# Expert weights in longer runs: two neighbouring rows to a partition, and a step of two on the stationary side

## The reference

```python
gate = jnp.minimum(xb @ wg + bg, SWIGLU_LIMIT)
up = jnp.clip(xb @ wu + bu, -SWIGLU_LIMIT, SWIGLU_LIMIT)
glu = gate * jax.nn.sigmoid(SWIGLU_ALPHA * gate)
return ((up + 1.0) * glu) @ wd + bd
```

## Time and profile before

| | |
|---|---|
| median of 3 runs | 1285.4 us |
| lowest and highest run | 1281.82 and 1287.41 us |
| span of the profiled execution | 1284.3 us |
| TensorE, matmuls busy | 1223.1 us (95%) |
| TensorE, weight loads busy | 552.0 us (43%) |
| VectorE, ScalarE, GpSimd busy | 250.6, 183.5 and 19.8 us |
| moved by DMA | 455.34 MB, 355 GB/s over the span |
| queue of the large loads | 132080 packets, 446.73 MB |

### The profile page before, as it was taken

How to read it: one execution, slowest core, us unless ns; L and a number is a source line. 1 busy time by engine, 2 the same in 40 slices (tenths; PEclk the granted TensorE clock), 3 DMA queues, 4 the chain that set the end, 5 groups by cost and what they waited for, 6 DMA issues and landing times.

```text
span 1284.3 us, 15147 instructions
## 1 busy us (share of the span) xinstructions
PE 1223.1 (95%) x6020; PEld 552.0 (43%) x6020; DVE 250.6 (20%) x535; ACT 183.5 (14%) x305; POOL 19.8 (2%) x40
## 2 busy tenths in 40 slices
PE   6699999999999999999999999999999999999995
PEld 1388965543333334443333333333333333333332
DVE  1334571511111111111111111111111111111113
ACT  1122431201111111111111111111111111111111
POOL 3000000000000000000000000000000000000000
PEclk9599999969999999999999999999999999999998
DMA  9994359529999999999999999999999999999971
GB/s 316 333 331 140 118 202 360 197 110 373 398 407 406 406 407 405 403 409 408 405 407 406 405 408 403 405 404 410 405 404 408 407 406 406 407 408 406 405 303 33
DMA packets 135160, 455.34 MB, mean 355 GB/s; under 512 B 7967, under 2 KB 21299, under 8 KB 135014
## 3 DMA queue, kind: packets, MB, share of 16 engines
q1 hardware_dynamic: 132080, 446.73, 89.3%
q0 software_dynamic: 2064, 6.98, 1.6%
q10 hardware_dynamic: 998, 1.37, 0.4%
HBM read 453.35 MB, written 1.70 MB: 354 GB/s over the span
## 4 chain that ended last, share of the span: by engine, by line
PE 82%; ACT 3%; DVE 1%; issue 0%
PE bank L1431 53%; PE bank L1415 10%; PE bank L1424 5%; PE bank L1441 5%; PE bank L1406 3%; PE bank L1307 2%; ACT k_pool L623 1%; PE bank L1102 1%; ACT at_pool L615 1%; PE bank L1134 1%; PE bank L1109 1%; PE bank L1463 0%; PE bank L1375 0%; PE bank L1343 0%; DVE xres L1063 0%; DVE k_pool L1062 0%
## 5 line engine op out<-in xcount | busy, mean ns | idle before, releaser
L1431 PE MATMUL bank<-ring,at_pool 128*64 128x512 f32 x2048 | 456.1, 598 | 0.0
L1431 PEld LDWEIGHTS bank<-ring,at_pool 128*64 128x64 f32 x2048 | 141.9, 137 | 310.5 <-issue 310.5
L1431 PE MATMUL bank<-ring,k_pool 128*64 128x512 f32 x1024 | 226.8, 595 | 23.0 <-ACT k_pool L623 23.0
L1431 PEld LDWEIGHTS bank<-ring,k_pool 128*64 128x64 f32 x1024 | 70.7, 137 | 158.5 <-issue 127.9
L1415 PEld LDWEIGHTS bank<-keyT,rows 128*128 128x128 f32 x1056 | 123.7, 196 | 28.6 <-issue 28.6
L1005 DVE TENSOR_SCALAR k_pool<-bank 128x512 f32<-128x512 f32 x32 | 22.1, 692 | 578.9 <-PE bank L1431 578.9
L1415 PE MATMUL bank<-keyT,rows 128*128 128x64 f32 x1056 | 128.5, 281 | 0.0
L615 ACT COPY at_pool<-bank 128x512 f32<-128x512 f32 x33 | 19.3, 586 | 443.3 <-PE bank L1415 443.3
L1424 PE MATMUL bank<-kv_pool,cumT 32*64 32x512 f32 x256 | 69.6, 620 | 0.0
L1009 DVE TENSOR_SCALAR k_pool<-bank 128x512 f32<-128x512 f32 x32 | 22.1, 692 | 226.9 <-PE bank L1431 226.9
L1441 PE MATMUL bank<-d_pool,at_pool 64*128 64x512 f32 x264 | 65.6, 615 | 0.7 <-ACT d_pool L625 0.7
(11 more groups left out here) (300 smaller groups left out, 590.5 us busy)
## 6 DMA issues: line engine op xcount, KB each, us to landing
ring<-in_w_gate SPq DMA_DIRECT2D x128, 1024.0 KB, 9.5
ring<-in_w_up SPq DMA_DIRECT2D x128, 1024.0 KB, 8.7
ring<-in_w_down SPq DMA_DIRECT2D x128, 1024.0 KB, 7.4
ring<-in_w_mod SPq DMA_DIRECT2D x24, 1024.0 KB, 10.1
ring<-in_w_in SPq DMA_DIRECT2D x13, 1024.0 KB, 12.5
ring<-in_w_out SPq DMA_DIRECT2D x4, 1024.0 KB, 6.7
k_pool<-in_const_masks POOLq DMA_DIRECT2D x1, 1024.0 KB, 8.0
g<-in_b_mod POOLq DMA_DIRECT2D x2, 512.0 KB, 12.3
```

Source lines behind the costliest of these rows:

```text
L1431: ins = mm(bank[CAP * half:CAP * (half + 1), :], lhsT(2 * r + kk), w[:, kk, 512 * half:512 * (half + 1)], start=m == 2 and r == 0 and kk = ...
```

## The change

A chunk of 256 rows is spread over the partitions in another way: partition p receives rows 2p and 2p + 1, which lie next to each other in memory, so that it reads one run of 8192 bytes where it read two of 4096. The slot then holds, as its two tiles, the even and the odd rows of the chunk. The two factors of each product have to agree on which features a tile holds, so the stationary side of the gather and of the transposes takes every second column of its 256: tile k is columns 256 * (k // 2) + k % 2, in steps of two. The number and the sizes of all transfers and instructions stay.

```diff
+        def pair_tile(k):
+
+            return slice(256 * (k // 2) + k % 2, 256 * (k // 2 + 1), 2)
+
...
                     sp.wait_ge(chunks_used, used(cidx - RING, count))
                     sp.dma_start(ring[:, expert_slot(cidx), :].rearrange("p (k n) -> p k n", k=2),
                                  w[0, bass.ds(e, 1), 256 * (cidx % 4):256 * (cidx % 4 + 1), :]
-                                 .rearrange("a (k p) n -> p (a k) n", p=P)).then_inc(slot_loaded[expert_slot(cidx)], 16)
+                                 .rearrange("a (p k) n -> p (a k) n", p=P)).then_inc(slot_loaded[expert_slot(cidx)], 16)
...
                     for t in range(2):
-                        ins = mm(B[3][:, CAP * k:CAP * (k + 1)], rows[:, t, P * k:P * (k + 1)], Ptok[:, t, :],
+                        ins = mm(B[3][:, CAP * k:CAP * (k + 1)], rows[:, t, pair_tile(k)], Ptok[:, t, :],
                                  start=t == 0, stop=t == 1)
...
                 for q in range(4):
-                    ins = tr(B[2][:, P * q:P * (q + 1)], ab[:, P * q:P * (q + 1)], ident)
+                    ins = tr(B[2][:, P * q:P * (q + 1)], ab[:, pair_tile(q)], ident)
```

## The result

The changed kernel takes 1292.3 us in the median of 8 runs (1287.0 to 1294.3), the kernel before 1286.1 in 8 runs of its own. The ratio is 1.0051 with a 95% interval of 1.003 to 1.0072: slower by some 6 us, where no change was forecast. It lies inside the range (1279 to 1304) and on the side that had a chance of 0.13.

What follows compares the result with a forecast made beforehand. The prediction took TensorE, busy 95% of the span, to bound the kernel. It summed 1284.3 + 0 (loads) + 0 (gather) + 0 (transposes) = 1284.3 us of span, with 1.1 to the median 1285.4 us; range 1279 to 1304.

Steps and rivals of the forecast that it cites:

- The term for the loads: Expert loads, 384 of 1 MB in 8192-byte runs: costed at nothing, covered by about 21 us of slack behind each load.
- 5.4 ns a load decide: Weight loads of gather and transposes: from 6.4 us / 1184 = 5.4 ns more per load, the slower rival decides.
- Equally bare: Transposes, right behind the gather: their four weight loads per expert, 0.48 us, were said to lie on the path without cover.
- VectorE's pair of rows: Recurrence on VectorE: 256 fp32 elements take 426 ns at a step of two, 425 ns in runs of 64 elements.
- The term's upper bound of 16 ns: Gather and transposes: ScalarE's 32 ns taken as the step's, 16 ns on 128 elements, 19 us over 1184 weight loads.
- The lower one: Gather and transposes: a non-contiguous order may cost or gain some 4 ns a weight load; that gain would be 5 us.
- the slower one by the weight loads: Gather and transposes: the step of two lengthens weight loads without cover; 1420 us at double read time; chance 0.08.
- double read time: Gather and transposes: each column takes twice its read time, 114 ns more a weight load, 135 us in all.
- The rival by the loads: Expert loads: new row order moves under 398 GB/s, TensorE waits for slots; 1315 us at 386 GB/s; chance 0.03.
- the one that the runs stay short: Expert loads: transfers are cut at 4096 bytes anyway, so loads are as today, 1285.4 us; chance 0.10.
- the one of less disturbance: Products: fewer, longer packets could disturb TensorE's reads less; faster, yet time that of today less chance; chance 0.02.

## Why the prediction was wrong

The reading of the bound held: the loop is bound by TensorE, a round is the sum of TensorE's pieces, and the loads have slack. The term for the loads was right at zero, and for the reason given; the loads alone give 0.999. So were the statements that the gather has no cover, that it goes at the pace of its weight loads, and that 5.4 ns a load decide. "Equally bare" was too much for the transposes, where ScalarE's copy covers part, and the first gather's loads, at half clock, paid nothing.

The step that failed is the one that priced a load: "I take 0, by VectorE's pair of rows, which has the same memory, element size and step." It is 6 ns for each of the 32 loads of a gather: 32 x 6 = 0.19 us a round, and 0.03 us more from the four loads of the transposes, 0.22 in all; over 31 rounds 6.8 us. VectorE's pair (425 and 426 ns for 256 elements) was no measure of TensorE's reading: VectorE takes 1.66 ns an element there, and by TensorE's own rate 8 bytes take 0.92, which would not show. (That VectorE reads at this rate no run shows; that a step of two costs it nothing, the loads without the step confirm.) A contiguous weight load takes 112 / 128 = 0.88 ns a column, less than those 0.92. No row of the trace of before could have told; what could have been seen is that VectorE, at nearly twice the time per element, could not show a price of that size. The term's upper bound of 16 ns held the 6 by luck: it is ScalarE's, which is no more a measure of TensorE's reading than VectorE's. The lower one came from the length of a load that reads one element again and again; lengths don't give the pace, and at a step of zero the pace is the contiguous one.

Of the rivals, the slower one by the weight loads is what happened, at a size of 6 ns, just over its point of decision, and not at double read time: at a step of two the price has only begun. Its 0.08 rested on the pairs of rows of VectorE and ScalarE, and beside its point of decision it was priced at double read time alone. Of its signs the gather over 3.9 us came (3.98); weight loads well over 196 ns did not (196 in the median). The rival by the loads falls (no wait, landings as before), the one that the runs stay short falls (half as many packets), and the one of less disturbance falls with them (products at 7.09 us in all runs at full clock).

No version beats the kernel before: the one with the loads alone is at 0.999 of it, with 1 inside the interval.

## What to carry to other kernels

When a stretch goes at the pace of weight loads, a stationary operand read at a step is priced by the stretches of 16 bytes that it touches. For the gather's 128 fp32 columns at full clock a step of two costs 5%, three 55%, four twice the time and eight no more than four, and it gets worse again if the slow stretch costs TensorE its clock. If a new data layout needs another order of features, put the order into an elementwise step that has room, or into the layout of small weights, and leave the stationary side contiguous, as the version with the loads alone does. And do not borrow the price of an access pattern from an engine that spends twice as long on an element.

## What the runs showed of the hardware

Not expected: a gather with weight loads 233 ns apart, in which TensorE is listed as busy without a gap, brings its granted clock from 1.00 to 0.50, and the product behind it pays 2.3 us each round. At 173 ns apart 18 rounds of 32 lose the clock and 14 keep it, and at 118 ns none does. Weight loads 233 ns apart keep that pace at either clock, while contiguous ones go from 112 to 211. And the same megabytes in half as many packets took 2% less of the DMA engines' time and moved no faster, because TensorE frees the slots; what runs of 8192 bytes could move with nothing else in the way, no run here shows.
